# Attention outputs computed as feature by token, with the values stationary and two heads on two column halves

## What is computed

```python
# per head: three branches over the same query
p_c = masked_softmax(q @ kc.T * scale + bias, ...)   # 31 compressed keys
p_s = masked_softmax(q @ ks.T * scale + bias, ...)   # selected keys: with 512 tokens, all earlier ones
p_w = masked_softmax(q @ kw.T * scale + bias, ...)   # window of 512: all earlier ones too
o = g[..., 0:1] * (p_c @ vc) + g[..., 1:2] * (p_s @ vs) + g[..., 2:3] * (p_w @ vw)
...
mix = jnp.concatenate([o, b_gate * conv(c_gate * x_t)], axis=-1) @ w_out
```

## Time and profile before

| | |
|---|---|
| Three runs | 1429.11, 1431.51, 1431.79 us; median 1431.51 us |
| Profiled execution, first to last instruction (span) | 1428.9 us |
| PE busy in the span | 1371.8 us (96%) |
| DVE busy | 698.6 us (49%) |
| ACT busy | 566.9 us (40%) |
| POOL busy | 465.6 us (33%) |
| Chain of work that ended last | PE 87%, DVE 7%, ACT 2% |

### The profile page before, as it was taken

How to read it: one execution, slowest core, us unless ns; L and a number is a source line. 1 busy time by engine, 2 the same in 40 slices (tenths; PEclk the granted TensorE clock), 3 DMA queues, 4 the chain that set the end, 5 groups by cost and what they waited for, 6 DMA issues and landing times.

```text
span 1428.9 us, 23064 instructions
## 1 busy us (share of the span) xinstructions
PE 1371.8 (96%) x9570; PEld 1131.4 (79%) x9570; DVE 698.6 (49%) x1192; ACT 566.9 (40%) x854; POOL 465.6 (33%) x131
## 2 busy tenths in 40 slices
PE   5999999999999999999999999999999999999998
PEld 3788766776788888888888678888798888888886
DVE  6656686464665333353337435687255454453002
ACT  4435654253342223222125445555364433443112
POOL 0243143024314434434522321121212443344344
PEclk9999999998999999999999999999999999999999
DMA  8763266002222232223214420011222223223311
GB/s 333 249 138 118 71 244 220 3 4 84 94 89 89 92 115 89 89 102 134 89 62 164 167 89 31 30 38 53 75 89 89 89 89 114 93 89 109 112 59 59
DMA packets 24741, 147.93 MB, mean 104 GB/s; under 512 B 2716, under 2 KB 3868, under 8 KB 9024
## 3 DMA queue, kind: packets, MB, share of 16 engines
q1 hardware_dynamic: 21128, 134.21, 26.6%
q10 hardware_dynamic: 3512, 12.26, 3.2%
HBM read 141.74 MB, written 4.72 MB: 103 GB/s over the span
## 4 chain that ended last, share of the span: by engine, by line
PE 87%; DVE 7%; ACT 2%; issue 2%; DMA 1%; POOL 1%; SPq 0%; DVEq 0%; ACTq 0%; POOLq 0%
PE bank L2090 24%; PE bank L2092 23%; PE bank L2091 23%; PE bank L2397 5%; PE bank L1168 2%; DMA raw<-in_weights 1%; PE bank L1159 1%; PE bank L1150 1%; DVE xres L1692 1%; PE bank L2276 1%; DVE act_lo L1689 1%; POOL xres L1330 1%; PE bank L2257 1%; DVE bank L1685 1%; PE bank L1077 1%
## 5 line engine op out<-in xcount | busy, mean ns | idle before, releaser
L1301 POOL TENSOR_TENSOR weight_lo<-raw,weight_hi 128x2048 fp32r<-128x2048 f32 (+2 forms) x90 | 415.1, 4612 | 822.9 <-ACT weight_hi L1349 822.8
L2090 PE MATMUL bank<-act_hi,weight_hi 128*128 128x512 f32 (+1 forms) x1136 | 433.1, 381 | 6.0 <-DVE q L879 1.9
L2092 PE MATMUL bank<-act_hi,weight_lo 128*128 128x512 f32 (+1 forms) x1136 | 422.8, 372 | 0.0
L2091 PE MATMUL bank<-act_lo,weight_hi 128*128 128x512 f32 (+1 forms) x1136 | 422.6, 372 | 0.0
L1349 ACT ACTIVATE weight_hi<-raw 128x2048 fp32r<-128x2048 f32 (+1 forms) x98 | 185.2, 1890 | 393.4 <-PE bank L2092 392.3
L2090 PEld LDWEIGHTS bank<-act_hi,weight_hi 128*128 128x128 f32 x1136 | 214.0, 188 | 48.0 <-issue 8.3
L2092 PEld LDWEIGHTS bank<-act_hi,weight_lo 128*128 128x128 f32 x1136 | 213.7, 188 | 38.6
L2091 PEld LDWEIGHTS bank<-act_lo,weight_hi 128*128 128x128 f32 x1136 | 214.1, 188 | 34.7 <-issue 0.5
L2090 PE MATMUL bank<-weight_hi,hid_hi 128*128 128x512 f32 x352 | 136.9, 389 | 0.0
L2091 PE MATMUL bank<-weight_lo,hid_hi 128*128 128x512 f32 x352 | 136.9, 389 | 0.0
L2092 PE MATMUL bank<-weight_hi,hid_lo 128*128 128x512 f32 x352 | 136.9, 389 | 0.0
(11 more groups left out here) (376 smaller groups left out, 1755.3 us busy)
## 6 DMA issues: line engine op xcount, KB each, us to landing
raw<-in_weights SPq DMA_DIRECT2D x120, 1024.0 KB, 4.8
w<-in_w ACTq DMA_DIRECT2D x2, 2048.0 KB, 12.0
bias_rows<-grow ACTq DMA_DIRECT2D x1, 2560.0 KB
xres<-in_x SPq DMA_DIRECT2D x4, 512.0 KB, 5.8
strip<-bias_rows ACTq DMA_DIRECT2D x1, 2048.0 KB, 9.8
out<-xres SPq DMA_DIRECT2D x3, 512.0 KB, 2.6
row_a<-in_ln_g ACTq DMA_DIRECT2D x2, 512.0 KB, 4.1
row_b<-in_ln_b ACTq DMA_DIRECT2D x2, 512.0 KB, 4.9
```

The costliest lines, as they stand in the source:

```text
L1301: pool.tensor_tensor(wlo[i % SPLIT][:, :size], raw[n % RAW][:, :size], whi[i % SPLIT][:, :size], ALU.subtract).then_inc(lo_ready, 1)
L2090: pe.matmul(o, l[0], r[0], start=first, stop=False)
L2091: pe.matmul(o, l[0], r[1], start=False, stop=False)
L2092: return pe.matmul(o, l[1], r[0], start=False, stop=last)
```

## The change

The order of the items becomes: for each pair of heads (2k, 2k+1) and tile i, [cmp for k = 0,] slc of both heads, win of both heads. The values are computed with the value matrix (128 keys by 64 features) stationary and the transposed probabilities (128 tokens) moving; head 2k writes PSUM rows 0 to 63 and head 2k+1 rows 64 to 127 of one bank, bank 4. All branches and tiles of a pair add up in that bank, so softmax sum and gate must be in the probabilities before they are turned: DVE scales the whole row of probabilities (128 x 128·(i+1)) by two per-row factors in place, and PE's transposes wait for that. The values step runs once for two items. The result lies feature by token, as the output product wants it: `turn_o`, its copies and subtractions go, and once for each pair ACT copies the bank to `out_hi` and DVE subtracts to `out_lo`. Scores and transposes rotate over three banks, 5 to 7, and the transposed probabilities over four buffers in place of two.

```diff
-ITEMS = [item for h in range(N_HEADS) for i in range(TT)
-         for item in ([("cmp", None, i)] if h == 0 else []) + [("slc", h, i), ("win", h, i)]]
+ITEMS = [item for k in range(PAIRS) for i in range(TT)
+         for item in ([("cmp", None, i)] if k == 0 else []) + [(br, 2 * k + c, i) for br in ("slc", "win") for c in range(2)]]
+HEAD_ITEMS = [n for n, item in enumerate(ITEMS) if item[0] != "cmp"]
+PROBS_AT = {n: at for at, n in enumerate(HEAD_ITEMS)}
+PAIR_END = [ITEMS.index(("win", 2 * k + 1, TT - 1)) for k in range(PAIRS)]
+TURNED = 4
...
+def second_of_pair(item):
+
+    return ITEMS[item][0] != "cmp" and ITEMS[item][1] % 2 == 1
...
-            if 0 <= slot - lag < len(ITEMS)]
+            if 0 <= slot - lag < len(ITEMS) and (st != "values" or second_of_pair(slot - lag))]
...
+    b.shared = range(5, 8)
...
+                if st == "values":
+                    b.add((st, item), 4, **(dict(act=1, dve=1) if item in PAIR_END else {}))
+                else:
+                    b.add((st, item), **(dict(act=1) if st == "turn2" else dict(dve=1)))
...
-    for k in range(PAIRS):
-        b.add(("turn_o", k), act=1, dve=1)
...
ACT, in a slot:
-                    if item >= 2:
-                        await_full(act, ("values", item - 2))
-                    b = bank(("turn2", item))
-                    a.done(act.activation(probsT[item % 2][:, 0:w], b[:, 0:w], ACT.Copy), drain(("turn2", item), "act"))
+                        n, w = PROBS_AT[item], n_keys(item)
+                        to = probsT[n % TURNED][:, 0:w]
+                        if n >= TURNED:
+                            reader = HEAD_ITEMS[n - TURNED]
+                            await_full(act, ("values", reader if second_of_pair(reader) else reader + 1))
+                    a.done(act.activation(to, bank(("turn2", item))[:, 0:w], ACT.Copy), drain(("turn2", item), "act"))
...
+                if slot - 3 in PAIR_END:
+                    name = ("values", slot - 3)
+                    await_full(act, name)
+                    a.done(act.activation(out_hi[:, PAIR_END.index(slot - 3), :], bank(name)[:], ACT.Copy), drain(name, "act"))
...
DVE, in a slot:
-                    stt(oh, bank(("values", item))[:, 0:HD], weights4[:, item % 4:item % 4 + 1], oh, ALU.mult, ALU.add,
-                        sem=drain(("values", item), "dve"))
+                if slot - 4 in PAIR_END:
+                    lo_of_pair(PAIR_END.index(slot - 4))
...
                     d.step(V.reciprocal(weights4[:, item % 4:item % 4 + 1], den[:, item % 3:item % 3 + 1]))
-                    ts(weights4[:, item % 4:item % 4 + 1], weights4[:, item % 4:item % 4 + 1],
-                       gate[:, i, 3 * h + part:3 * h + part + 1], sem=S["weight_ready"])
+                    ts(probs, probs, weights4[:, item % 4:item % 4 + 1], gate[:, i, 3 * h + part:3 * h + part + 1],
+                       ALU.mult, ALU.mult, sem=S["weight_ready"])
...
+        def lo_of_pair(k):
+
+            name = ("values", PAIR_END[k])
+            await_drained(dve, name, "act")
+            tt(out_lo[:, k, :], bank(name)[:], out_hi[:, k, :].bitcast(F32), ALU.subtract, sem=drain(name, "dve"))
...
PE, in a slot:
-                    pe.wait_ge(S["exp_done"], item + 1)
+                    pe.wait_ge(S["weight_ready"], PROBS_AT[item] + 1)
...
-                        mm = pe.matmul(b[:, 0:HD], probsT[item % 2][:, tok(j)],
-                                       (vsl if br == "slc" else vwn)[:, j, HD * (h // REP):HD * (h // REP) + HD],
-                                       start=j == 0, stop=j == i)
+                        for c, x in enumerate(pair):
+                            mm = pe.matmul(b[head_of(c), tok(i)], values[:, j, HD * (h // REP):HD * (h // REP) + HD],
+                                           probsT[PROBS_AT[x] % TURNED][:, tok(j)], start=(br, j) == ("slc", 0), stop=(br, j) == ("win", i))
+                    if br == "slc":
+                        if h == 1:
+                            await_drained(pe, ("turn2", CMP_AT[i]), "act")
+                        for c in range(2):
+                            n = N_KV * ((h - 1 + c) % REP) + h // REP
+                            mm = pe.matmul(b[head_of(c), tok(i)], vc4[:, n % (2 * N_KV), :], cmpT[:, i, tok(n // (2 * N_KV))],
+                                           start=False, stop=False)
...
-        for k in range(PAIRS):
-            claim(pe, ("turn_o", k))
-            await_drained(pe, ("values", len(ITEMS) - 1), "dve")
-            for t in range(TT):
-                mm = pe.transpose(bank(("turn_o", k))[:, tok(t)], o[:, t, P * k:P * k + P], ident[:])
-            fill(("turn_o", k), mm)
...
-        dense_rows("mix2", "out2", 4, (act_hi, act_lo),
-                   ready={0: (S["y2_lo"], 2), 1: (S["y2_lo"], 4), 2: drained_at(("turn_o", 1), "dve"),
-                          3: drained_at(("turn_o", 3), "dve")}, turned=True,
+        dense_rows("mix2", "out2", 4, [(act_hi, act_lo)] * 2 + [(out_hi, out_lo)] * 2,
+                   ready={0: (S["y2_lo"], 2), 1: (S["y2_lo"], 4), 2: drained_at(("values", PAIR_END[1]), "dve"),
+                          3: drained_at(("values", PAIR_END[3]), "dve")}, turned=True,
```

More of the change, by code:

```diff
@@ L420, in plan_second @@
             for st, item in stages_of(slot):
-                by_act = st == "turn2" or (st == "values" and ITEMS[item][0] == "cmp")
-                b.add((st, item), **(dict(act=1) if by_act else dict(dve=1)))
-    for k in range(PAIRS):
-        b.add(("turn_o", k), act=1, dve=1)
+                if st == "values":
+                    b.add((st, item), 4, **(dict(act=1, dve=1) if item in PAIR_END else {}))
+                else:
+                    b.add((st, item), **(dict(act=1) if st == "turn2" else dict(dve=1)))
+    b.shared = range(4, 8)
     dense_rows("mix2", "out2_3", act=1)
@@ L564, in build @@
     cgT = here("cgT", [P, 4, SEQ])
+    strip_at = nxt
     strip = here("strip", [P, N_HEADS, SEQ])
-    o = here("o", [P, TT, MIX])
+    out_parts, _ = place("attention_out", [P, N_HEADS, SEQ], F32R, strip_at)
+    out_hi, out_lo = (out_parts[:].rearrange("p (k a) n -> p a k n", a=2)[:, part] for part in range(2))
+    turned_probs = here("turned_probs", [P, 2, SEQ])
+    cmpT = here("turned_cmp", [P, TT, 2 * P])
     blk = here("blk", [P, L_CMP // 2, N_KV * CMP_W])
@@ L759, in second_act @@
                drain(("turn_v", "gates"), "act"))
-        for n, name in enumerate(SLOT_UNITS):
+        for n, unit in enumerate(SLOT_UNITS):
             convert()
@@ L779, in second_act @@
                                               scale=-1.0, accum_out=den[:, x:x + 1]), S["exp_done"])
[L780 to L786, removed]
+                if slot - 3 in PAIR_END:
+                    name = ("values", slot - 3)
+                    await_full(act, name)
+                    a.done(act.activation(out_hi[:, PAIR_END.index(slot - 3), :], bank(name)[:], ACT.Copy), drain(name, "act"))
+            if unit[:2] == "cg":
                 for j in range(2):
-                    await_full(act, (name, j))
-                    a.done(act.activation(cgT[:, 2 * int(name[2]) + j, :], bank((name, j))[:], ACT.Copy), drain((name, j), "act"))
+                    await_full(act, (unit, j))
+                    a.done(act.activation(cgT[:, 2 * int(unit[2]) + j, :], bank((unit, j))[:], ACT.Copy), drain((unit, j), "act"))
         act.wait_ge(S["upper_free"], 1)
@@ L987, in second_dve @@
                         continue
[L988 removed]
+                    part, probs = ("cmp", "slc", "win").index(br), scores[item % 3][:, 0:n_keys(item)]
                     d.step(V.reciprocal(weights4[:, item % 4:item % 4 + 1], den[:, item % 3:item % 3 + 1]))
[L990 to L991 removed]
+                    ts(probs, probs, weights4[:, item % 4:item % 4 + 1], gate[:, i, 3 * h + part:3 * h + part + 1],
+                       ALU.mult, ALU.mult, sem=S["weight_ready"])
             if name[:2] == "xt":
@@ L1006, in second_dve @@
             lo_of_convolution(k)
-        for k in range(PAIRS):
-            await_full(dve, ("turn_o", k))
-            await_drained(dve, ("turn_o", k), "act")
-            tt(act_lo[:, k, :], bank(("turn_o", k))[:], act_hi[:, k, :].bitcast(F32), ALU.subtract, sem=drain(("turn_o", k), "dve"))
+        lo_of_pair(PAIRS - 1)
         def add_rms(stage, e, t, row, between=()):
@@ L1139, in attention @@
                 b = bank((st, item))
-                claim(pe, (st, item))
+                if st != "values" or (br, i) == ("slc", 0):
+                    claim(pe, (st, item))
                 if st == "scores" and br == "cmp":
```

36 lines of the change are left out of this document (12 added, 24 removed).

## The result

| | before | changed |
|---|---|---|
| Median of the runs | 1431.0 us (1429.1 to 1431.8, 4 runs) | 1461.6 us (1457.2 to 1462.1, 4 runs) |
| Ratio, 95% interval | 1 | 1.0205 (1.0176 to 1.0234) |
| Span of the profiled run | 1428.9 us | 1460.2 us |
| Stage, first scores to last values | 843.68 to 1004.48, 160.8 us | 843.04 to 1036.25, 193.2 us |

The forecast was 1453.6 us, 22.1 above before; measured are 30.6 by the medians and 31.3 by the spans. The stage alone grew by 32.4 us, the end behind it shrank by 1. The time lies inside the range that was given 8 chances in 10, 1433 to 1467 us, and 0.6 us above the forecast's own range of 1446 to 1461.

What follows compares the result with a forecast made beforehand. PE was taken to set the attention stage's pace, DVE and ACT less than a slot ahead. Terms -6.8 + 11.3 + 2.1 + 16.5 - 1.0 = +22.1 on 1431.5 gave 1453.6 us; own range 1446 to 1461, 8 in 10: 1433 to 1467.

Steps and rivals of the forecast that it cites:

- the forecast's own range: Whole kernel: 1446 to 1461 us, from entries of 0 to 0.38 us and waits of 0.4 to 0.6.
- PE's load, -6.8: Values product on PE: 32.4 us against 39.2, with column halves running at once and 0.38 us for each of 32 visits.
- The new wait, +11.3: PE's transposes wait for DVE's scaled row behind head_scores: 23 slots of 0.49 us each.
- lo_of_pair, +2.1: DVE's pair-end subtraction between head_scores and the scaling delays the transposes three times, 0.72 us each.
- The scaling meets POOL, +16.5: DVE's wide scaling stops while POOL makes weight_lo: five PE waits, 20.8 us, less overlaps; bounds 0 and 23.
- The end, -1.0: From last dense group to output product: nine steps, 6.5 us in place of 7.5.
- One sign: What would show the forecast right: PE's busy time in the stage falls by some 7 us while the stage grows by 23.
- The rival of compounding waits (1467): Waits feed on each other as DVE leaves POOL stops with work still queued: +14, 1467 us; chance 0.12.
- Free: three banks in place of four: Scores and transposes on three banks cost nothing: a bank's previous content is a slot and a half old, drained.

Runs made afterwards that it cites:

- experiment 1: Changed kernel without the wide scaling: DVE makes only the 128x1 weight, transposes wait for the exponential alone; 1416.0 us, ratio to before 0.9896.
- experiment 2: Changed kernel with POOL's six weight_lo subtractions of the stage issued in 8 pieces each; 1432.4 us, ratio 1.0003.
- 3: Changed kernel with 16 additional matmuls in front of the waiting transposes in each of the five stops, keeping PE busy; 1446.7 us, ratio 1.0115.
- experiment 7: Changed kernel with POOL's weight_lo in 8 pieces, and the values product without column halves, 128 stationary columns for each head; 1444.7 us, ratio 1.0091.
- experiments 4: Changed kernel with DVE's slot turned round: reciprocal and wide scaling of the previous item before head_scores; 1455.9 us, ratio 1.0185.
- experiment 5: Changed kernel with transposes and values one slot later and a fourth buffer of probabilities; 1432.3 us, ratio 0.9993.
- experiment 11: Changed kernel with transposes a slot later and POOL in 8 pieces, plus slc and win values in one visit a tile; 1415.8 us, ratio 0.9889.
- experiment 9: Kernel before the change with POOL's six weight_lo of the stage in 8 pieces, nothing else; 1426.9 us, ratio 0.9968.

## Why the prediction was right, and where it fell short

Kernels 1, 2 and 3 lie on a line from before to the changed kernel, each one cause apart. By stage length, and what of it is the opening at half clock:

| step | stage, us | opening | rest | medians | prediction |
|---|---|---|---|---|---|
| before to 1: cheaper values, no new wait | 160.8 to 151.3, -9.5 | -1.7 | -7.8 | -15.3 | -6.8, end -1.0 |
| 1 to 2: the short waits | to 165.1, +13.8 | +3.4 | +10.4 | +16.4 | +11.3 + 2.1 |
| 2 to 3: five standstills, at full clock | to 179.3, +14.2 | -3.4 | +17.6 | +14.3 | +16.5 |
| 3 to changed: the clock behind them | to 193.2, +13.9 | +3.4 | +10.5 | +14.9 | nothing |

- **PE's load, -6.8: right,** and measured as 7.8 us (8.0 by span times clock over the runs). The sum itself is 0.2 us off: 35.5 and 3.5 are 39.0, not 39.2. Concurrency holds at 128 columns: the weight loads of the two halves start together (timeline of the changed kernel, below), and the pairs of the visit follow each other every 0.109 us. The visit is 0.26 to 0.35 us by experiment 7, not 0.38.

```profile
1032.00 0.13 PEld L1177 LDWEIGHTS bank<-acc,vsl 128*64 128x64 f32 x1 [0.17 <-issue]
...
1032.01 0.13 PEld L1177 LDWEIGHTS bank<-sc,vsl 128*64 128x64 f32 x1
```

- **The new wait, +11.3, and lo_of_pair, +2.1: right in kind, 1.5 to 3 us too much in size.** 13.4 us were forecast; without the opening the stage gives 10.4, the runs by span times clock 11.9. The rows of experiment 2 have 18 waits, 9.6 us together, where 23 of the one kind and three of the other were counted. The chain from scores to scaling does end behind PE, by 0.53 us on average. What `lo_of_pair` costs was not measured apart.
- **The scaling meets POOL, +16.5: right in kind and nearly in size.** PE stands idle in the five stops for 3.5 to 4.0 us, 18.7 us together, where 20.8 were forecast; as a step they cost 17.6 us by the stage, 14.5 by span times clock over the runs.
- **The end, -1.0: right:** it measures 6.4 us where 6.5 were forecast.
- **What failed is the sum's silent assumption that a standstill costs its own length.** No term stood for the clock. The rows could have given it: the earlier trace rows show 0.50 before the change, in a window ahead of which PE had waited 1.6 us (up to 809.87), and the prediction itself had five new standstills of some 4 us. The clock behind the stops measures 10.5 us by the stage without the opening, 14.9 by the medians, 14.6 by the windows: the largest miss. The four terms that the sum did have come to 19.2 us (-7.8, +10.4, +17.6, -1.0) against 22.1, so the load came out better and the waits shorter than forecast, and that hid part of the missing term.
- **The range held by luck.** The bounds given for the forecast's own range (entries 0 to 0.38 us, waits 0.4 to 0.6) make 1439.7 to 1456.1 us by the same sum, not 1446 to 1461, and none of them stands for the clock. 1461.6 lies in the wide range because that range was drawn up to 1467 for compounding waits, which did not come.
- **One sign did not show.** PE's busy time in the stage was to fall by 7 us; it rose from 155.1 to 165.3, since the same work takes longer at half clock. In experiment 1 it falls to 146.2.
- **The clock by the skill.** The Trainium skill (TensorE: Matmul & The Clock Gate, Part 1: The HAM clock gate) says that PE falls to half clock when idle and has to be busy again for a while before it gets the full one; by this the cost of a stop is its length and half of the slow stretch behind it. The trace agrees, with 0.50 in 917.8 to 923.0.
- **The rival of compounding waits (1467) was near the measured time, but by another mechanism.** Outside the five stops PE never waited longer than 1.0 us for the scaling in the changed kernel; its 13 short waits sum to 6 us.
- **"Free: three banks in place of four"** holds for the changed kernel as it is: its transposes go 0.15 us behind the scaled row. Once the chain is moved (experiments 4 and 5) they go 0.39 to 0.79 us behind it, when the bank is drained: a quarter to two thirds of a microsecond for a wait, and not the reason of the long stops.

Open: why one execution loses some microseconds of clock ahead of the stage and in its opening and another doesn't; and what a visit costs by experiment 11, within runs that spread by 12 us.

## What to carry to other kernels

A wide SBUF-to-SBUF operation that is put on DVE between two PE steps should be looked up against POOL's instructions: here six long ones cost 29 us of 1461. With one slot more of slack, and either POOL's instructions in eight pieces or the scaling given to ACT, the same change is 0.9 to 1.1% faster than before. Price a new PE standstill of a few microseconds with the clock behind it, which here cost 10 to 15 us beside the 17.6 of the five standstills. And when a chain is moved, look up what drains the banks that come next: it came last in experiments 4 and 5, though by less than 0.7 us a wait. Before a difference of a few microseconds is given to an edit, compare the clock of the two profiles.

## What was not expected of the hardware

- PE's clock: all five standstills of 3.5 to 4.0 us were followed by stretches of 3.5 to 12.9 us with a mean of 0.50 to 0.63. In experiment 5, PE's waits of 3.1 and 2.1 us were followed by half clock (0.56 and 0.76 in the 7 us behind), waits of 2.0 and 2.8 us were not, so the length of the wait alone doesn't decide:

```profile
901.00:908.00 7.00, 6.92 (x24) 5.33 (x25) 3.39 (x16) 2.49 (x9) 0.00 (x0) 0.56 0.45 152
...
931.00:938.00 7.00, 6.83 (x40) 5.73 (x41) 4.81 (x21) 3.26 (x11) 0.00 (x0) 0.76 0.44 150
...
959.00:966.00 7.00, 6.79 (x47) 5.26 (x47) 6.40 (x22) 4.57 (x11) 0.00 (x0) 1.00 0.43 151
...
986.60:994.00 7.40, 7.21 (x53) 5.72 (x53) 6.07 (x24) 4.85 (x13) 0.00 (x0) 1.00 0.42 142
```

- A DVE operation is stopped even when its record begins first: in experiment 5 the scaling's record begins at 895.93, POOL's at 895.96, and the scaling, 0.35 us when undisturbed, takes 4.63 us.
- Eight pieces of POOL's subtraction cost it little: 0.78 us each with their meetings, 6.2 us for a unit in place of 4.6. The kernel before isn't slower with them (experiment 9).
